# The seams between sections: the second RMS statistic from cross products, adds to x by accumulating transfers, and VectorE's work in chunk order

## The reference

```python
def _rmsnorm(x, g):
    y = x * rsqrt(mean(x * x, axis=-1, keepdims=True) + EPS)
    return y * g

def _pre(x, g, mod, k):
    return _rmsnorm(x, g) * (1.0 + mod[:, 3 * k + 1]) + mod[:, 3 * k]

def _post(x, y, g, mod, k, weight):
    return x + weight * mod[:, 3 * k + 2] * _rmsnorm(y, g)

x = _post(x, _swiglu(_pre(x, g[0], mod_lat, 0), ffn1_gu, ffn1_down), g[1], mod_lat, 0, 0.5)
h = _pre(x, g[2], mod_lat, 1) @ w_in
...                                   # the mixer gives y from h
x = _post(x, y, g[3], mod_lat, 1, 1.0)
x = _post(x, _swiglu(_pre(x, g[4], mod_lat, 2), ffn2_gu, ffn2_down), g[5], mod_lat, 2, 0.5)
```

## Time and profile before

| | |
|---|---|
| median of three runs | 2648.77 us (2648.14 to 2652.62) |
| the profiled execution | 2646.27 us |
| its span | 2644.5 us |
| mean granted clock of TensorE | 0.998 |
| TensorE busy | 2586.2 us, 98% |
| VectorE busy | 1596.0 us, 60% |
| ScalarE busy | 714.7 us, 27% |
| POOL busy | 816.1 us, 31% |

### The profile page before, as it was taken

The page is one execution under the profiler, slowest core; times in us unless marked ns, Lnnn a source line. Parts: engine busy times, 40 slices in busy tenths (PEclk is TensorE's granted clock), DMA queues, the critical chain, the costliest instruction groups (busy, mean ns, idle before and its releaser), DMA issues.

```text
span 2644.5 us, 40750 instructions
## 1 busy us (share of the span) xinstructions
PE 2586.2 (98%) x17044; PEld 2429.9 (92%) x17044; DVE 1596.0 (60%) x2238; ACT 714.7 (27%) x1050; POOL 816.1 (31%) x1286
## 2 busy tenths in 40 slices
PE   6999999999999999999999999999999999999998
PEld 5999999998989899999999899999999878888886
DVE  6688878766574676676676633433343684544443
ACT  4222212123334411212113412122122424322223
POOL 1278876832140100000001148667651131000001
PEclk9999999999999999999999999999999999999999
DMA  9534444453364234434432422222223565233331
GB/s 338 154 123 156 157 143 133 161 187 132 117 194 144 79 98 136 130 108 138 136 104 91 109 67 83 94 92 90 94 88 116 189 196 163 72 96 96 96 96 64
DMA packets 346831, 334.54 MB, mean 127 GB/s; under 512 B 52496, under 2 KB 319896, under 8 KB 343576
## 3 DMA queue, kind: packets, MB, share of 16 engines
q1 hardware_dynamic: 284344, 198.19, 25.7%
q10 hardware_dynamic: 52288, 77.20, 8.7%
q0 software_dynamic: 10016, 56.56, 5.6%
HBM read 287.40 MB, written 44.50 MB: 126 GB/s over the span
## 4 chain that ended last, share of the span: by engine, by line
PE 86%; DVE 8%; POOL 2%; issue 1%; ACT 1%; DMA 1%; SPq 0%; DVEq 0%; POOLq 0%; ACTq 0%
PE ps L473 81%; POOL xT L1282 1%; DVE tmpN L1496 1%; DVE hL L1500 1%; PE ps L1302 1%; PE ps L1317 1%; DVE zb L2105 1%; DVE zd L2106 1%; PE ps L1050 1%; ACT wH L458 1%; PE ps L1069 1%; DVE zc L2118 0%; PE ps L1326 0%; DVE SR L2122 0%; PE ps L1702 0%
## 5 line engine op out<-in xcount | busy, mean ns | idle before, releaser
L473 PE MATMUL ps<-hH,wH 128*128 128x384 f32 (+1 forms) x2928 | 1013.5, 346 | 8.5 <-DVE hL L1500 8.0
L473 PE MATMUL ps<-hH,wL 128*128 128x384 f32 (+1 forms) x2928 | 1004.9, 343 | 0.0
L473 PE MATMUL ps<-hL,wH 128*128 128x384 f32 (+1 forms) x2928 | 1004.5, 343 | 0.0
L465 DVE TENSOR_TENSOR wL<-raw,wH 128x1024 fp32r<-128x1024 f32 x300 | 396.4, 1332 | 493.2 <-ACT wH L458 491.7
L473 PEld LDWEIGHTS ps<-hH,wH 128*128 128x128 f32 x2928 | 549.9, 188 | 35.4 <-DVE hL L1500 7.4
L473 PEld LDWEIGHTS ps<-hH,wL 128*128 128x128 f32 x2928 | 550.1, 188 | 18.1
L473 PEld LDWEIGHTS ps<-hL,wH 128*128 128x128 f32 x2928 | 550.2, 188 | 17.8
L473 PE MATMUL ps<-midH,wH 128*128 128x384 f32 (+1 forms) x1232 | 424.0, 344 | 2.9 <-DVE yT L948 2.5
L473 PE MATMUL ps<-midH,wL 128*128 128x384 f32 (+1 forms) x1232 | 421.5, 342 | 0.0
L473 PE MATMUL ps<-midL,wH 128*128 128x384 f32 (+1 forms) x1232 | 421.3, 342 | 0.0
L458 ACT ACTIVATE wH<-raw 128x1024 fp32r<-128x1024 f32 x300 | 310.9, 1049 | 366.2 <-PE ps L473 349.5
(11 more groups left out here) (284 smaller groups left out, 2261.3 us busy)
## 6 DMA issues: line engine op xcount, KB each, us to landing
...
x_d<-xT POOLq DMA_DIRECT2D x4, 3072.0 KB, 11.2
xT<-x_d POOLq DMA_DIRECT2D x4, 3072.0 KB, 10.6
...
```

Source lines behind the costliest of these rows:

```text
L465: nc.vector.tensor_tensor(wL[:, n % SPLIT_SLOTS, :], raw[:, n % RAW_SLOTS, :], wH[:, n % SPLIT_SLOTS, :].bitcast(f32), ALU.subtract).then_ ...
L473: ins = nc.tensor.matmul(dst, a, b, start=first and n == 0, stop=last and n == 3 * len(pairs) - 1)
```

## The change

The second statistic is no longer taken from the new x. With z = P·y, r the first statistic's reciprocal root and P the gain, the new x is x + r·z, and the sum of its squares is the old sum of x², plus 2·r times the sum of x·z, plus r² times the sum of P²·y². The kernel keeps the sum of x² (`sumX`) from seam to seam.

- `statP` holds 1 and the squares of the two gains as weights of the sums of y², so one pass gives three rows: y² and P²y² for context and latent. TensorE makes the sums of the first chunks between the matmuls of the last chunks (`square_sums`); POOL's running sum is left out in all but the last section.
- VectorE multiplies x·z per chunk right behind the last adds (`cross_z`, L1483) and adds chunks 1 to 5 into chunk 0; TensorE sums the three that are left (`cross_sums`). `new_sums` puts the three terms together on six columns.
- VectorE adds chunk 0 alone to x. For chunks 1 to 7 POOL issues accumulating transfers of yT into xT (L1363), each behind the scaling of its chunk. The scaling reads the spread statistic from `rowY`, which ScalarE copies to SBUF.
- `joined_vector` does VectorE's work in chunk order: scale x of chunk m, scale y of chunk m + 2 (m + 3 in the latent seam), low part of chunk m.
- `first_groups` takes all eight chunks in chunk order, and three units in a mixer too; the state inputs come one unit later. The head weights stand behind the second spread in other banks. SP loads two more units first and waits for five chunks of h before it loads states.
- The wait for x from DRAM moves ahead of the last adds. The norm behind the last section is as before, but that VectorE and POOL add four chunks each.

```diff
-        lead = KC - 3
+    def first_groups(pe, base, count, pre, between=None, cw_ready=None):
+
+        lead = KC if pre.after else KC - 3
         order = [(k, u) for k in range(lead) for u in range(count)]
         order += [(k, u) for u in range(count) for k in range(lead, KC)]
         for k, u in order:
             if u == 0:
                 pe.wait_ge(h_lo, KC * pre.nth + k + 1)
+            if k == 0:
+                pe.wait_ge(w_lo, base + u + 1)
+                if u == 1 and cw_ready:
+                    pe.wait_ge(cw, cw_ready)
+                if u == 2:
+                    pe.wait_ge(row_y, pre.after.nth + 1)
...
+    def cross_sums(pe, S, m):
+
+        pe.wait_ge(cross_x, cross_count(S, m))
+        return row_sums(pe, 6, crossed(S, m), S.tok0, TOK, m == 0, m == KC - 1)
+
+    def square_sums(pe, S, m, t0, t1, first=False, last=False):
+
+        return row_sums(pe, 7, sq[:, m, :], t0, t1, first, last, statP[:, m, :])
...
+            while S.next and m >= 2 and summed < m:
+                pe.wait_ge(sq_y, KC * S.post.nth + summed + 1)
+                square_sums(pe, S, summed, S.tok0, TOK, summed == 0)
+                summed += 1
...
+                ins = cross_z(dve, S, m, token_segments(S.tok0))
+                if 0 < m < CROSS_SUMMED:
+                    dlink(dve, ins)
+                    dsync(dve)
+                    ins = nc.vector.tensor_tensor(crossed(S, 0)[:, S.tok0:TOK], crossed(S, 0)[:, S.tok0:TOK],
+                                                  crossed(S, m)[:, S.tok0:TOK], ALU.add)
+                if m < CROSS_SUMMED - 1:
+                    dlink(dve, ins)
+                else:
+                    ins.then_inc(cross_x, 1)
...
-    def post_pool(pool, N):
+    def post_pool(pool, N, S):
         wait_back(pool, N)
-        for m in POOL_CHUNKS:
+        if not N.has_next:
+            for m in range(LAST_POOL):
+                pool.wait_ge(y_norm, KC * N.nth + m + 1)
+                add_to_x(pool, nc.gpsimd, N, m, x_new)
+            return
+        for m in range(1, KC):
             pool.wait_ge(y_norm, KC * N.nth + m + 1)
-            add_to_x(pool, nc.gpsimd, N, m, x_new_pool)
-
-    def row_sums(pe, bank, squares, t0, t1, first, last):
+            pool.dma_start(xT[:, m, N.tok0:TOK], yT[:, m, N.tok0:TOK], accum_op=ALU.add).then_inc(x_added[m - 1], 16)
...
+    def post_tensor(pe, N, S):
+        if S.next is None:
+            end_sums(pe, N, S)
+            return
+        nxt = S.next
+        pe.wait_ge(sq_y, KC * N.nth + KC - 2)
+        square_sums(pe, S, KC - 3, N.tok0, TOK)
+        if N.tok0 == 0:
+            for m in (KC - 2, KC - 1):
+                pe.wait_ge(sq_half, 2 * N.nth + m - (KC - 2) + 1)
+                square_sums(pe, S, m, 0, HALF)
+        for m in (KC - 2, KC - 1):
+            pe.wait_ge(sq_y, KC * N.nth + m + 1)
+            ins = square_sums(pe, S, m, N.tok0 or HALF, TOK, False, m == KC - 1)
+        ins.then_inc(ss_y, 1)
+        for m in (0, KC - 2, KC - 1):
+            ins = cross_sums(pe, S, m)
+        ins.then_inc(ss_x, 1)
+        pe.wait_ge(rs_y, N.nth + 1)
+        spread_matmuls(pe, 4, 5, N.tok0, rstd, bc_y, bc_y_ctx)
+        keep_clock(pe, 2)
...
+        pre_spread(pe, nxt)
         if S.tag.startswith("f1"):
             head_weights(pe, S.gen)
-        else:
-            keep_clock(pe, 10)
-        wait_x(pe, N, 0)
         keep_clock(pe, 3)
+        pe.wait_ge(h_tmp, KC * nxt.nth + 1)
+        keep_clock(pe, 2)
+        pe.wait_ge(h_hi, KC * nxt.nth + 1)
...
+            root(act, rstdX[:], sumX[:], N.tok0, sum_x, N.nth + 1, sd_x)
+            act.wait_ge(y_norm, KC * N.nth + 1)
+            for t0, t1, v in token_segments(N.tok0):
+                ins = nc.scalar.activation(rowY[:, t0:t1], seg_ps(4, 5, v), ACT.Copy)
+            ins.then_inc(row_y, 1)
...
+    def new_sums(dve, N, S):
+
+        b = N.tok0 // 128
+        r, d, c, x = (t[:, b:6] for t in (rstd, sumD, cross, sumX))
+        dve.wait_ge(rs_y, N.nth + 1)
+        for b0, b1, v in [(b, 2, CTXV), (2, 6, LAT)][b // 2:]:
+            dlink(dve, nc.vector.tensor_tensor(sumD[:, b0:b1], turnedY[:, b0:b1, 1 + v], rstd[:, b0:b1], ALU.mult))
+        dsync(dve)
+        dlink(dve, nc.vector.tensor_tensor(d, d, r, ALU.mult))
+        dsync(dve)
+        dlink(dve, nc.vector.tensor_tensor(x, x, d, ALU.add))
+        dve.wait_ge(ss_x, N.nth + 2)
+        columns(dve, 6, N.tok0, cross).then_inc(cols_x, 1)
+        dve.wait_ge(cols_x, N.nth + 2)
+        dsync(dve)
+        dlink(dve, nc.vector.scalar_tensor_tensor(d, c, 2.0, r, ALU.mult, ALU.mult))
+        dsync(dve)
+        dlink(dve, nc.vector.tensor_tensor(x, x, d, ALU.add))
+        dsync(dve)
+        nc.vector.tensor_scalar(x, x, 0.0, None, ALU.max).then_inc(sum_x, 1)
...
+    def joined_chunk(dve, post, N, m, ahead):
+
+        dve.wait_ge(h_lo, KC * N.nth + m - 1 if m >= 2 else KC * N.nth + 1)
+        wait_x(dve, post, m)
+        for t0, t1, v in token_segments(N.tok0):
+            ins = scaled(N, m, t0, t1, v)
+        ins.then_inc(h_tmp, 1)
+        if m + ahead < KC:
+            scale_y(dve, post, m + ahead)
+        rest(dve, N, m)
...
+    def joined_vector(dve, post, N, late):
+
+        c, l = token_segments(0)
+        dve.wait_ge(bc_y_ctx, post.ctx_nth + 1)
+        dsync(dve)
+        dlink(dve, scale_part(post, 0, *c, seg_ps(4, 5, CTXV)))
+        inverse_x(dve, N)
+        dve.wait_ge(bc_y, post.nth + 1)
+        scale_part(post, 0, *l, seg_ps(4, 5, LAT)).then_inc(y_norm, 1)
+        dsync(dve)
+        dlink(dve, add_part(*c[:2]))
+        dve.wait_ge(y_norm, KC * post.nth + 1)
+        add_part(*l[:2]).then_inc(x_new, 1)
+        dve.wait_ge(bc_x_ctx, N.nth + 1)
+        dsync(dve)
+        scaled(N, 0, *c).then_inc(h_tmp_ctx, 1)
+        dve.wait_ge(row_y, post.nth + 1)
+        scale_y(dve, post, 1)
+        dve.wait_ge(bc_x, N.nth + 1)
+        wait_x(dve, post, 0)
+        scaled(N, 0, *l).then_inc(h_tmp, 1)
+        scale_y(dve, post, 2)
+        dve.wait_ge(h_hi_ctx, N.nth + 1)
+        low(0, *c)
+        dve.wait_ge(h_hi, KC * N.nth + 1)
+        low(0, *l).then_inc(h_lo, 1)
+        for n in late:
+            split_lo(dve, n)
+        for m in range(1, KC):
+            joined_chunk(dve, post, N, m, 2)
...
         sp.wait_ge(w_used, M.base)
+        load_units(RAW_SLOTS, 5)
+        sp.wait_ge(h_lo, KC * pre.nth + 5)
         load_states(0)
         load_states(1)
         load_phases(0)
-        load_units(RAW_SLOTS, 5)
         sp.wait_ge(h_lo, KC * pre.nth + KC)
         load_phases(1)
+        load_units(5, 7)
...
-        first_groups(pe, M.base, 2, pre)
+        first_groups(pe, M.base, 3, pre, None, M.gen.n0["cw"] + 1)
...
-        for m in range(2, 8):
+        for m in range(3, 8):
             proj(m)
-            if m >= 2 and m < 6:
-                state_inputs(m - 2)
+            if m < 7:
+                state_inputs(m - 3)
```

276 lines of the change are left out of this document (164 added, 112 removed).

## The result

The changed kernel takes 2660.1 us, the median of eight runs (2653.0 to 2665.3), against 2648.7 of the kernel before beside it: the ratio is 1.0034, with an interval of 1.0018 to 1.0051. It is slower; 2622 was forecast. The profiled execution took 2665.3 us (span 2663.5), 5 above the median, and the mean granted clock was 0.988, in the eight runs 0.987 to 0.991, where it was 0.998 before. The trace of the kernel before is of one of its fastest executions (2646.3 us; its runs beside the experiments reach from 2645.8 at a mean clock of 0.998 to 2657.7 at 0.994), so the two traces differ by 19 us where the medians differ by 11.

The account below looks back on a forecast made before the run. The bound was taken as TensorE's chain of waits at the five seams. Gains 2 × 6.45 + 5.0 + 3.5 + 3.5 + 2.2 = 27.1 us, less 1.0 for late transfers, gave 2620.2 profiled, 2622 as median; range 2611 to 2644.

Parts of the forecast that it names:

- E: End of the old section's last matmul; five sums on TensorE make it 2.3 us later, 1.8 in the latent seam.
- The seam: From the old section's last projection to the next section's first: about 11.0 us against 22.5, 9.4 in the latent seam.
- The steps: First groups of a section: each chunk's scaled x, high part and low part follow each other in 3.4 us.
- the landing: Time of an accumulating transfer of y into x, seven per seam: taken as 4.1 us, in time up to about 4.5.
- rival B: Transfers land partly late, at 4.8 to 5.7 us; a full seam loses 2 to 6 us, time 2629 to 2647; chance 0.13.
- The rival's formula: Loss of a full seam at landing L: 3.5 × (L − 4.5) + (L − 3.9), half the excess per chunk.
- The mixer's gain of 6.45: Each of two mixers' seams: fourth unit starts at +41.8 against 50.55 us, less 2.3, a gain of 6.45 us.
- rival D: A later wait (state inputs, spilled x, held loads) eats the mixers' gain; run at 2637 us; chance 0.06.
- Tz: TensorE's two waits in the mixers for these output tables, 2.3 us in all, the longer 1.7; 2.2 were to go.
- The clock: TensorE's clock may fall in the seams; a fall costs up to 1.7 us, most of it absorbed by slack.
- A's range: Range of the forecast case itself, 2611 to 2632 us, chance 0.68; small operations, last adds and Tz waits may vary.
- FFN seams: Seams into the FFNs: gains of 3.5 us behind the first mixer, 5.0 in an FFN, 3.5 in the latent seam.

Follow-up runs that it names:

- e1: The changed kernel with the loads of a mixer's first two state matrices and phases issued at the end of the section before: 2651.1 us, ratio 0.9999.
- g1: The changed kernel with y of a full seam scaled three chunks ahead instead of two, so transfers are issued one step sooner: 2649.7 us, ratio 0.9989.
- f2: The changed kernel with only the store of x put behind the first chunks of u: 2661.2 us, ratio 1.0031.
- f1: The changed kernel with the first state matrix loaded early, second matrix and phases behind all chunks, store of x behind the first chunks of u: 2660.8 us.
- g3: The changed kernel with y scaled three chunks ahead, the store of x in two halves and the first state matrix loaded early: 2643.8 us, ratio 0.9967.
- h1: g3 with four clock-keeping products behind chunk 0 and four ahead of the fourth unit of every seam: 2639.3 us, ratio 0.9959.

## Why the prediction was wrong

- **E.** Five sums were to cost 2.3 us (1.8 latent). Measured, the last projection came 3.1 us later in the four full seams and 2.6 in the latent one: 0.8 too little in each.
- **The seam** from there: right, 10.56 for 11.0, and 9.14 for 9.4. The small operations, the spreads and the order of chunk 0 came as worked out.
- **The steps**: 3.4 us, right wherever no transfer was late. At chunk 1 the steps leave TensorE a wait of 1.5 us (1.2 + 3.4 − 3.12); it waited 1.3 to 2.0 in three seams and 3.6 in the second mixer's. In f11's it did not wait there; its first products ran at half clock.
- **The step that failed** is the landing: "I take 4.1", one number for all 35 transfers, and the reason given against rival B, that "the change holds most of these loads until chunk 5". Alone a transfer took 3.9, as taken. But five chunks are not eight: with 2.75 MB issued at the fifth, chunk 7's landed in 9.5 and 10.7 us. At both mixers' seams that is 4.6 and 5.8 us of TensorE's waiting. e1, which takes the loads away, and g1, which only issues the transfers earlier, both took these waits away, and g1 is 12 us faster. The rival's formula would not have priced this place either: it charges half of a landing's excess over 4.5 us per chunk, 2.5 and 3.1 here, since two chains of chunks alternate; behind the last chunk there is no other chain, and nearly the whole excess of 5.0 and 6.2 us was paid. I had spread a late landing over all chunks of all seams, and so given it 0.13 as a whole kernel and nothing at one place.
- **The mixer's gain of 6.45, "twice",** had a second hole: the store of x, which lay in the old seam's cover, moves behind the last transfer and meets u. The state inputs' waits of 3.4 and 2.7 us are in no term of the sum. That is rival D's mechanism, at 0.06. f2 showed the store to be a source, f1 that the place behind the first chunks of u is no better; g3, with 1 MB less to load, brought the waits to 1.6 and 2.4, so the loads have a part in them.
- **Tz**: 2.2 us were to go; it waited 4.5 in the second mixer. In g3, with the mixer's start eased, it waited 1.5; in h1 1.7. Why it came late in some kernels and not in others stays open.
- **The clock**: "inside A's range" was wrong. The prediction priced a fall at up to 1.7 us, by the one of 3.41 us that it had seen, and took most of it as absorbed by slack. There were nine falls, with 51 us at half clock, and the longest, 13.66 us behind Tz, lay where TensorE has no slack and cost 6.4 us.
- **FFN seams**: gains of nothing, 3.3 and 2.1 us for 3.5, 5.0 and 3.5. E has 0.8 of the missing part in each; the rest is transfers of 4.5 to 5.0 us that were late by some tenths (bound 4.5), and in f20 two falls, one of which cost 1.7. The table load there showed: its fourth unit waited 2.0, f11's 1.1.
- **The sum**: E (3.9), the two last chunks (10.4), chunk 1 of the second mixer (2.1), the state inputs (6.1), Tz (4.4 against the forecast), the fall behind it (6.4) and that in f20 (1.7) make 35 of the 45 us by which the profiled execution (2665.3) missed the forecast for it (2620.2). That none of them hides another is an assumption; the other 10 stay open.
- With the causes eased (h1), the ratio of 0.9959 is 2638 us in the terms of the forecast, still 16 over it. E (4), the first state inputs (2.4 and 2.0) and Tz (1.7) account for 10; the rest stays open.

The Trainium skill's estimate of the landing, 2.0 + 2 × 0.9 = 3.8 us ("DMA: Bandwidth & Descriptors", section "Anatomy of one DMA — SWDGE (gpsimd) path", and "Collectives: The Full Stack", section "The bandwidth ceiling: the fold count and why AG ≠ RS ≠ AR"), agrees with the 3.9 of a transfer alone; beside the loads 9.5 and 10.7 were measured.
